# A decoder layer on one core: modulation sums moved from TensorE to VectorE, six PSUM banks for the jobs, w2 in column halves

## The reference

```python
mod = silu(c) @ w_ada + b_ada                       # six rows of 1024: sh1, sc1, gt1, sh2, sc2, gt2
h = rmsnorm(x, norm1) * (1 + sc1) + sh1
da_q, da_k, da_v, ml_qk, ml_v, ml_o, ml_if, g_a, g_m = split(h @ w_in)
y_a = diff_attention(...)                           # 4 heads, causal, ALiBi
y_m = rmsnorm(sigmoid(ml_o) * mlstm(...))           # 4 heads, ml_qk through a causal convolution
merged = sigmoid(g_a) * (y_a @ w_br_a) + sigmoid(g_m) * (y_m @ w_br_m)
x = x + gt1 * (merged @ w_out)
h2 = rmsnorm(x, norm2) * (1 + sc2) + sh2
x = x + gt2 * hier_moe(h2, ...)                     # best of 4 groups, best 2 of its 8 experts, 32 experts in all
return rmsnorm(x, norm_f)
```

## Time and profile before

| | us |
|---|---|
| three runs: median (lowest to highest) | 477.31 (475.33 to 478.41) |
| profiled execution, its own time | 477.03 |
| its span, first to last instruction | 475.2 |
| TensorE busy | 404.6 (85%) |
| ScalarE busy | 187.6 (39%) |
| VectorE busy | 168.3 (35%) |
| GpSimd busy | 157.2 (33%) |
| DMA moved | 164.3 MB, mean 346 GB/s |
| mean granted TensorE clock | 0.952 |

### The profile page before, as it was taken

The page is one execution under the profiler, slowest core; times in us unless marked ns, Lnnn a source line. Parts: engine busy times, 40 slices in busy tenths (PEclk is TensorE's granted clock), DMA queues, the critical chain, the costliest instruction groups (busy, mean ns, idle before and its releaser), DMA issues.

```text
span 475.2 us, 8601 instructions
## 1 busy us (share of the span) xinstructions
PE 404.6 (85%) x3612; PEld 310.7 (65%) x3612; DVE 168.3 (35%) x350; ACT 187.6 (39%) x344; POOL 157.2 (33%) x125
## 2 busy tenths in 40 slices
PE   6499999999898999999996989989795595866944
PEld 5399999987788999989975635445362261542611
DVE  0987257795028420492254030211211103011023
ACT  4667555762993394435253303131212021120212
POOL 0699776765447559996100000000000000000000
PEclk9799999998999999999999989999998898797996
DMA  8999998579887455479998899999999999999912
GB/s 280 425 419 422 420 420 325 177 268 360 348 319 281 154 210 196 165 297 421 426 419 350 319 355 425 421 419 421 419 422 421 420 419 423 419 420 420 422 74 90
DMA packets 23657, 164.32 MB, mean 346 GB/s; under 512 B 2624, under 2 KB 2752, under 8 KB 4928
## 3 DMA queue, kind: packets, MB, share of 16 engines
q1 hardware_dynamic: 23184, 162.15, 84.2%
q10 hardware_dynamic: 432, 1.57, 0.9%
HBM read 162.67 MB, written 1.05 MB: 344 GB/s over the span
## 4 chain that ended last, share of the span: by engine, by line
PE 66%; DMA 20%; ACT 4%; DVE 4%; SPq 3%; issue 2%; DVEq 0%; ACTq 0%
PE bank L1327 17%; PE cs_b L1327 9%; PE cs_b L1667 8%; DMA gm<-in_e 6%; DMA ring<-in_e 6%; DMA his<-in_e 6%; PE bank L1370 5%; PE bank L1635 5%; PE bank L1678 5%; PE bank L1624 4%; SPq L441 3%; PE cs_b L1280 3%; PE bank L1375 2%; DMA hT<-in_xT 2%; PE cs_b L1624 1%
## 5 line engine op out<-in xcount | busy, mean ns | idle before, releaser
L483 POOL TENSOR_TENSOR ring_r<-ring,his_r 128x512 fp32r<-128x512 f32 x120 | 156.9, 1343 | 59.1 <-ACT his_r L507 59.1
L741 ACT ACTIVATE raw<-bank,sm 128x128 f32<-128x128 f32 x72 | 27.2, 457 | 152.4 <-PE bank L1635 152.4
L507 ACT ACTIVATE his_r<-ring 128x2048 fp32r<-128x2048 f32 (+1 forms) x32 | 57.7, 1803 | 30.2 <-DMA ring<-in_rest 13.9
L1667 PE MATMUL cs_b<-ring,raw 128*32 128x256 f32 x544 | 51.2, 401 | 6.7 <-DMA ring<-in_e 6.7
L1206 DVE TENSOR_TENSOR tmp<-cs_b,tmp 128x256 f32<-128x256 f32 x8 | 3.4, 424 | 123.0 <-ACT tmp L749 123.0
L1667 PEld LDWEIGHTS cs_b<-ring,raw 128*32 128x32 f32 x544 | 26.9, 115 | 21.9 <-issue 11.7
L1635 PEld LDWEIGHTS bank<-const,xn 128*128 128x128 f32 x288 | 34.2, 191 | 10.1 <-issue 7.1
L1635 PE MATMUL bank<-const,xn 128*128 128x128 f32 x288 | 36.1, 278 | 2.7 <-ACT raw L741 1.6
L1678 PE MATMUL bank<-ring,WT 128*32 128x512 f32 x112 | 30.3, 693 | 4.8 <-DMA gm<-in_e 3.2
L1327 PE MATMUL bank<-his_r 128*128 128x256 f32 x208 | 29.8, 286 | 0.0
L1624 PE MATMUL bank<-v,const 128*128 128x512 f32 x54 | 26.4, 628 | 3.4 <-issue 3.4
(11 more groups left out here) (391 smaller groups left out, 849.3 us busy)
## 6 DMA issues: line engine op xcount, KB each, us to landing
ring<-in_e SPq DMA_DIRECT2D x48, 1024.0 KB, 26.1
ring<-in_rest SPq DMA_DIRECT2D x40, 1024.0 KB, 9.3
his<-in_e SPq DMA_DIRECT2D x17, 1024.0 KB, 26.2
ring<-in_block SPq DMA_DIRECT2D x8, 768.0 KB, 21.5
late<-in_e SPq DMA_DIRECT2D x5, 1024.0 KB, 20.3
qkT<-in_e SPq DMA_DIRECT2D x5, 1024.0 KB, 24.4
mqk<-in_e SPq DMA_DIRECT2D x5, 1024.0 KB, 26.1
gm<-in_e SPq DMA_DIRECT2D x4, 1024.0 KB, 22.3
```

The lines of the kernel that those rows point to most:

```text
L483: pool.tensor_tensor(ring_r[:, slot_of(n), sl], ring[:, slot_of(n), sl], hi(d)[:, sl].bitcast(F32), ALU.subtract).then_inc(s["w_lo"], 1)
L507: act.activation(hi(d)[:, 0:WIDTH[d]], ring[:, slot_of(n), 0:WIDTH[d]], ACT.Copy).then_inc(s["w_hi"], 1)
L741: ins = act.activation(xg[:, b, k, :], token_bank[:, j * P:(j + 1) * P], ACT.Identity, bias=S("B2", KD)[:, k:k + 1], scale=S("A2", KD)[:, ...
L1667: ins = pe.matmul(up_bank[e * CAP:(e + 1) * CAP, half], xg[:, b, k, e * CAP:(e + 1) * CAP], wt[e][:, k, :], start=(k == 0), stop=(k == KD ...
```

## The change

1. **Modulation sums.** The four `ada` groups are no longer products on TensorE. Their units are w_ada transposed, 256 columns each, and VectorE multiplies and sums them (`sums_of(i, u)`: two 128x1024 passes a unit against `cs_b`) into `m2`; `columns` adds the bias. gt1 and gt2 are spread over the partitions by four small matmuls a half (`gate_rows`), and VectorE copies them. The two bias DMAs go. The slot of an `ada` unit is free when its sum is done. The units are interleaved one by one with the dense ones.
2. **Banks.** `cs_b` stays occupied until after the branch products, so the jobs up to there run on banks 0 to 5.
3. **Start.** xT is one DMA of 8 KB rows ahead of `const`; VectorE squares half of it.
4. **First gather** in two banks (`g1`), and `up` with w1 waits for its second half only from k = 4 on. `turn`, the second `gate_rows` for gt2 and its copy move behind that `up`.
5. **w2 units** hold two experts' columns of one half instead of one expert's all. `down` waits and raises `used` by halves, and VectorE's products with `gt2b` follow by halves.
6. `w_r` is scaled by one instruction instead of eight; TensorE loads the flag before the last quad.

```diff
 def unit_list():
-    units += w_in(C_MQK, 4) + w_in(C_MV, 2) + ada(3) + w_in(C_MO, 1) + ada(4) + w_in(C_MO + 256, 1)
-    units += w_in(C_GA, 1) + ada(2) + w_in(C_GA + 256, 3) + w_in(C_GM, 4)
-    units += [("br_a", 0), ("br_a", 512), ("br_m", 0), ("br_m", 512)] + ada(5)
+    units += w_in(C_MQK, 4) + w_in(C_MV, 2) + ada((3, 0)) + w_in(C_MO, 1) + ada((3, 1), (3, 2)) + w_in(C_MO + 256, 1)
+    units += ada((3, 3)) + w_in(C_GA, 1) + ada((4, 0), (4, 1)) + w_in(C_GA + 256, 1) + ada((4, 2), (4, 3))
+    for i, c0 in enumerate((C_GA + 512, C_GA + 768, C_GM, C_GM + 256, C_GM + 512, C_GM + 768)):
+        units += w_in(c0, 1) + ada((2, i) if i < 4 else (5, i - 4))
+    units += [("br_a", 0)] + ada((5, 2)) + [("br_a", 512)] + ada((5, 3)) + [("br_m", 0), ("br_m", 512)]
...
-BANK, TURN = {}, {}
-for _name, _bank in FIRST_JOBS + [(n, (6 + i) % 8) for i, n in enumerate(JOBS)]:
-    BANK[_name], TURN[_name] = _bank, sum(b == _bank for b in BANK.values())
+TAIL = (("wo0", None), ("wo1", None), ("wo2", 6), ("x2T0", 7), ("x2T1", None), ("wo3", None), ("x2T2", None), ("lg", None),
+        ("x2T3", None), ("rank", 7), ("gt2b0", None), ("g1", 6), ("gt2b1", 7))
+BANK, TURN, HELD = {}, {}, [0] * 8
+for _name, _bank in FIRST_JOBS + [(n, None) for n in JOBS] + list(TAIL):
+    if _bank is None:
+        _bank = sum(_n in JOBS or (_n, None) in TAIL for _n in BANK) % 6
...
-RELEASES = [(LATE, "ymT1"), (LAST[0], "brm1"), (QKT, "brm3"), (LAST[1], "brm3")] + [(i, "ada5") for i in LAST[2:6]]
+RELEASES = [(LATE, "ymT1"), (LAST[0], "bra1"), (LAST[1], "sum15"), (LAST[2], "bra3"), (LAST[3], "sum16"), (LAST[4], "brm1"),
+            (QKT, "brm3"), (LAST[5], "brm3")]
...
         def _(sp):
+            sp.dma_start(hT[:].rearrange("p k n -> p (k n)"), t["xT"]).then_inc(xT_in, 16)
             sp.dma_start(const[:, 0:NFRONT], t["const"][:, 0:NFRONT]).then_inc(const_in, 16)
-            for i in range(2):
-                sp.dma_start(hT[:, 4 * i:4 * i + 4, :].rearrange("p k n -> p (k n)"), t["xT"][:, 1024 * i:1024 * i + 1024]
-                             ).then_inc((xT0_in, xT1_in)[i], 16)
...
+            def sums_of(i, u):
+                n = UNITS.index(("ada", (i, u)))
+                dve.wait_ge(landed[slot_of(n)], landed_value(n))
+                for a in range(2):
+                    w, at = slot(slot_of(n))[:, a * D:(a + 1) * D], 8 * (i - 2) + 2 * u + a
+                    ins = dve.tensor_tensor_reduce(w, w, cs_b[:], 1.0, 0.0, ALU.mult, ALU.add, m2[:, at:at + 1])
+                ins.then_inc(s["sums"], 1)
+                dve.wait_ge(s["sums"], ADA.index(n) + 1)
...
             mix(3)
-            columns(B2, 3)
-            dve.tensor_copy(S("B2_r", KD), B2).then_inc(s["mod2"], 1)
+            sums_of(3, 0)
+            sums_of(3, 1)
             dve.wait_ge(*full("cols"))
...
             for h in range(HEADS):
                 decay_arg(h)
-            rows(4)
-            columns(A2, 4)
-            rows(2)
+            sums_of(3, 2)
+            sums_of(3, 3)
+            columns(B2, 3).then_inc(s["mod2"], 1)
             dve.wait_ge(s["h_sq"], 1)
...
+            for u in range(4):
+                sums_of(4, u)
+            link(columns(A2, 4))
...
-            for k in range(KD):
-                dve.tensor_scalar(w_r[:, k, :], w_r[:, k, :], A2[:, k:k + 1], None, ALU.mult).then_inc(s["wr_r"], 1)
+            dve.tensor_tensor(w_r[:], w_r[:], A2.unsqueeze(2).to_broadcast([P, KD, G + NE]), ALU.mult).then_inc(s["wr_r"], 1)
...
             for i in range(4):
+                sums_of(5, i)
                 job, view = f"bra{i}", ga[:, 2 * i:2 * i + 2, :]
                 dve.wait_ge(*full(job))
                 release(dve.tensor_tensor(view, pb(job)[:].rearrange("p (a n) -> p a n", a=2), view, ALU.mult), job)
+            columns(S("G2", KD), 5).then_inc(s["gate_c"], 1)
+            for i in range(2):
+                release(dve.memset(S("fence", 2)[:, i:i + 1], 0.0), f"cs{i}")
...
             def quad(q, it, b):
-                dve.wait_ge(used, it * QU + QU)
                 for c in range(2):
+                    dve.wait_ge(used, it * QU + UP_UNITS + 2 * c + 2)
...
             dve.tensor_copy(ptg[:, 0].rearrange("p t n -> p (t n)"), token_bank[:, 0:T]).then_inc(s["pt_evac"], 1)
+            spread(gt2b, 2, (1,))
...
+            def gate_rows(g, half):
+                ps = take(f"gt{g}b{half}")
+                pe.wait_ge(s["gate_c"], g)
+                for j in range(4):
+                    k = 4 * half + j
+                    ins = pe.matmul(ps[:, j * P:(j + 1) * P], S(f"G{g}", KD)[:, k:k + 1].to_broadcast([P, P]), ident,
+                                    start=True, stop=True)
+                filled(ins, f"gt{g}b{half}")
...
             def up(w, r, j, b):
+                    if k == KD // 2 and isinstance(r, int) and r + j == 0 and w == "w1":
+                        pe.wait_ge(s["g_evac"], 2)
...
             def down(r, j):
-                wt = [arrived("w2", e, r, j) for e in range(QUAD)]
                 for c in range(2):
+                    wt = [arrived("w2", 2 * c + pair, r, j) for pair in range(2)]
...
-                            if c == 1 and f == 1:
+                            if f == 1 and e % 2 == 1:
                                 ins.then_inc(used, 1)
...
             def quad(r, j):
                 up("w1", r, j, b)
+                if first:
+                    pe.wait_ge(s["pg_ready"], 1)
+                    turn(False)
+                    gate_rows(2, 1)
...
             gather(0)
-            pe.wait_ge(s["g_evac"], 1)
-            gather(1)
-            pe.wait_ge(s["g_evac"], 2)
-            pe.wait_ge(s["pg_ready"], 1)
-            turn(False)
-            for job in ("rank", "gt2b0", "gt2b1"):
-                pe.wait_ge(*free(job))
+            gather(1, take("g1"))
+            pe.wait_ge(*free("gt2b0"))
             for q in range(NQ):
+                if q == NQ - 1:
+                    pe.wait_ge(s["flag_r"], 1)
+                    over = pe.value_load(flag[0:1, 0:1], min_val=0, max_val=1)
                 quad(q // LOOP, q % LOOP)
-            pe.wait_ge(s["flag_r"], 1)
-            over = pe.value_load(flag[0:1, 0:1], min_val=0, max_val=1)
```

More of the change, by code:

```diff
@@ L55, in unit_list, with ada @@
 def unit_list():
-    def ada(i):
-        return [("ada", (i, k)) for k in range(0, KD, 2)]
+    def ada(*parts):
+        return [("ada", part) for part in parts]
     def w_in(c0, n):
@@ L71, in unit_jobs @@
 def unit_jobs():
[L73 to L76 removed]
+    jobs = [f"ml{i}" for i in range(4)] + ["mv0", "mv1", "mo0", "mo1"] + [f"ga{i}" for i in range(4)]
+    jobs += [f"gm{i}" for i in range(4)] + ["bra1", "bra3", "brm1", "brm3"] + [f"wo{i}" for i in range(4)]
+    jobs = iter(jobs)
+    return [None if kind in ("mod", "block", "ada") else next(jobs) for kind, _ in UNITS]
 UNITS = unit_list()
@@ L951, in _ @@
             mix(1)
-            rows(3)
             gate_sums()
@@ L1091, in residual @@
                 own(dve.tensor_tensor(xv, xv, tv, ALU.add), "x2", i + 1)
-            rows(5)
+            spread(gt1b, 1)
+            dve.wait_ge(*free("gt1b1"))
             for i in range(4):
```

168 lines of the change are left out of this document (63 added, 105 removed).

## The result

The changed kernel takes 480.17 us (median of 4 runs, 479.88 to 481.47), the kernel before beside it 476.32 us. The ratio is 1.0119, 95% interval 1.0078 to 1.016. (The two medians alone lie 0.8% apart.) In a second set, nine runs against 23 of before, the ratio was 1.0093 (1.0061 to 1.0124). In some executions any kernel is slower (the longest took 819.56 us); the ratios and intervals leave these out. The profiled execution took 479.88 us with a span of 478.1, against 475.2 before.

A forecast was written before the change was run, and what follows sets the result against it. TensorE bounds the kernel until quad 0 frees its w3 slots, then full DMA queues do. +1.4 - 8.1 + 0.9 + 2.3 + 1.7 - 0.65 - 2.1 = -4.5 us gave 473 us (-0.9%), range 465 to 480.

The forecast's parts named there:

- the middle: From `ml0` to `gm0`: taking three `ada` products off TensorE gains 8.1 us, or -7.2 with +0.9 for slow clock.
- The start: Up to the first products: `const` waits behind xT, lands at 6.0 us and costs 1.4 us.
- step 1: Around `mix(3)`: it ends at 110.2 us as before, then two modulation sums run until 115.0.
- third rival: Whole kernel: GpSimd slows VectorE's passes, 0.46 us more per pass giving 482 us; chance 13%.
- Steps 2 to 4: Up to `num0`: `ga2`'s weights land near 122.3 us, `o` products end at 133.6, `num0` can start at 145.3.
- Step 3: From ScalarE's split of `ga2`'s weights to VectorE's end of the `o` products: 11.3 us as before, until 133.6.
- step 4: Ahead of `num0`: four sums take 9.6 us, then A2, `rbias`, `w_r` and `decay(0)` 2.1, until 145.3.
- The clock before `num0`: TensorE's slow clock after a 3.9 us wait before `num0`: +0.9 us, half the +1.7 taken before `wo0`.
- The merge: From `y_low` to `wo0`: VectorE's sums cost +4.6 us, additions meeting an idle GpSimd save 2.3; net +2.3.
- the second: Whole kernel: TensorE's six new waits, each followed by 1.2 GHz, eat the gain; 477 us, no change; chance 22%.
- Quad 0: First gather to w3's end: w1 ends about 258.8 instead of 262.84, but w3, which counts, gains only 0.65 us.
- The tail: Last quad: `down` starting before the last w2 unit -1.0, a hidden `gt2b` product -0.6, flag load 0.5; sum -2.1 us.

The follow-up runs named there:

- the best kernel: Changed kernel with constants first, GpSimd held back at three places, decays ahead of the sums, and the 128x8 sum behind the merge: 461.19 us, ratio 0.9698.

## Why the prediction was wrong

It said 473.0 us, -0.9%; the time rose by 1.2%. The range, 465 to 480, just missed 480.17. The step that failed is the middle: -7.2 us with its clock term, -0.4 measured. The sum carried the times of VectorE's old instructions over as they were, although the change gives them other neighbours on GpSimd.

- **The start** was mis-sized: +1.4 predicted, +2.8 measured. `const` landed at 6.2 us as said (6.0), but `cs` took 3.78 us instead of 3.50 and `ss` 4.41 where I put 3.9 (it varies by more than a microsecond between the profiles), and the first `normalize` behind it met GpSimd (1.44 us for 0.69).
- **The middle, step 1**: "`mix(3)` ends at 110.2 as before". It ended at 115.0. Of these 4.8 us, 2.8 are the start's delay. Most of the other 2.0 are GpSimd's: the gate sums took 4.8 us more and, as most of its row now lies ahead of it, `mix(3)` with its reciprocal and scaling 3.2 us less. The rule on two SBUF inputs was at hand in my third rival, and I used it to clear the new passes, rightly, but not to go through the old instructions whose neighbours changed.
- **Steps 2 to 4**: `ga2`'s weights reached ScalarE at 128.58 and not at 122.3, 1.4 us more than the start and step 1 explain; it is a landing time that was put too short. Step 3 came out (11.2 us for 11.3). `num0` started at 153.01 and not at 146.7 (145.3 with the start's cost), as step 4's small instructions took 3.6 us, not 2.1, again beside GpSimd. That the sums of step 4 hold `num0` was right, as the kernel with the decays ahead of them shows: it is also the point where the change could be mended.
- **The clock before `num0`**: +0.9 predicted, 2.8 measured. I halved it because matmuls precede the wait closely; they didn't help. (The wait was put at 3.9 us, though the steps give 145.3 - 141.8 = 3.5; it was 4.57.) Before `wo0` +1.7 predicted, 2.6 measured. Together, 2.0 (step 1, net), 1.4 (landing), 1.5 (small instructions) and 1.9 us (clock) make up the 6.8 us that the middle lacks.
- **The merge**: from `y_low`'s end to the first `brm` product 12.9 us (12.7 predicted), from there to `wo0` 8.1 instead of 12.87, a relief of 4.8 where I took 2.3. That part was better than said. But `y_low` in front of it cost 3.8 us more, and no step had it. This part is a draw: with nothing held at that place the pair took 7.04 us in four profiles of changed kernels and 3.25 or 3.27 in two.
- **The rivals**: the second, the gain eaten by waits and slow clock, was right in kind on the clock but had the waits too short, and the 5.11 us one ahead of the gate rows wasn't among them. The third, at 482 us, was nearest in number and right that GpSimd slows VectorE, but on the wrong instructions: the passes kept their 1.21 us. No rival had the two together.
- **Quad 0**: -0.65 predicted, -0.95 measured; w1 was through in 7.4 us (7.8 in the sum). That nothing after quad 0 gives time back was right: in the best kernel `wo0` is 18.1 us earlier than in the changed one and the last `down` 18.6.
- **The tail**: -2.1 predicted, in the last two rows of the table together, -4.4 measured there. The last row's -2.1 is no proof of its -1.1. The wait between VectorE's end and the scatter was peculiar to the profiled run of before, and its scatter ran at half clock; against the kernel with x first, whose tail is the old one (16.0 us from the last `down`'s start to the end), the changed kernel's 16.7 is no gain. Of my three terms only `down` starting ahead of the last w2 unit is borne out: it follows `turn` by 0.9 us, without the 1.45 us wait for a transfer, where it took 1.8 before.

## What to carry to other kernels

When work moves between engines, list the two-operand SBUF instructions of VectorE on the path and look at what GpSimd does beside each of them in the new order: the moved work can be free and its new neighbours ruinous. If GpSimd has slack, hold its row back with one semaphore wait at the few places that matter, and look at what its row then meets. And where a slower engine now serves the faster one, put its new work behind what the fast one waits for; that was worth more here (9 us) than any other single edit.

## What the runs showed of the hardware that I had not expected

- A VectorE instruction of 128x8 elements with two SBUF operands can last 8.30 us, one of 128x512 18.5 us, until GpSimd's unbroken row ends. With GpSimd's work in smaller pieces the longest wait was longer (in the one profile taken) and the usual one shorter (7.5 to 4.9 us for five).
- While VectorE was shut out, GpSimd lost nothing: 16 pieces in 20.07 us, 1.25 us each. Where VectorE got in between, GpSimd paid too: 8 pieces in 11.46 us beside the gate sums, 1.43 us each.
- Tiny instructions suffer like large ones, and not only those that read two tensors: the scaling of 128x2 elements by a scalar held in SBUF (L920), with a single tensor as input, took 1.07 and 1.13 us beside GpSimd and 0.23 us in its pause; the reciprocal of 128x4 ahead of it took 0.17 us in both. Why the one waits and the other doesn't no run here shows.
- A VectorE pass with one operand in SBUF and one in PSUM took 1.20 to 1.22 us in all 13 profiles of kernels with the sums on VectorE, beside GpSimd or not.
